# ScalarE loads one table set for Exp and Ln, and other sets at written places, in a two-block transformer kernel

## The reference

```
rms_norm:        x * rsqrt(mean(x*x) + eps) * g           (Sqrt; or Ln, then Exp)
recurrence:      log_f = logaddexp(log_lb, log1p(-lb) + log_sigmoid(fr))
                 k_in  = (1 - lb) * sigmoid(-fr)           (Exp, Ln; Sigmoid)
                 decay = exp(differences of cumsum(log_f))  (Exp)
attention:       softmax                                    (Exp)
stick-breaking:  log_beta = log_sigmoid(z)
                 log_1m   = where(mask, log_sigmoid(-z), 0)
                 after    = cumsum(log_1m, reverse) - log_1m
                 a        = exp(log_beta + after)           (Exp, Ln; Exp)
feed-forward:    (silu(h @ w_gate) * (h @ w_up)) @ w_down   (Silu)
gates:           sigmoid(...)                               (Sigmoid)
rotary tables:   cos, sin                                   (Sin)
```

## Time and profile before

| | before |
|---|---|
| median of 3 runs | 1090.27 us (1089.99 to 1090.49) |
| span of the profiled execution | 1087.6 us |
| TensorE (PE) busy | 1062.6 us, 98% |
| VectorE (DVE) busy | 748.0 us, 69% |
| ScalarE (ACT) busy | 599.6 us, 55% |
| table loads (ACT_TABLE_LOAD) | 36, 46.2 us |

### The profile page before, as it was taken

One profiled execution on the slowest core, in us unless ns is written; L12 is line 12 of the kernel. 1 busy time (PEld: TensorE's weight loads), 2 busy tenths in 40 slices (PEclk: granted clock), 3 DMA queues, 4 the chain that ended last, 5 costly groups with the idle time before them and its releaser, 6 DMA issues.

```text
span 1087.6 us, 22291 instructions
## 1 busy us (share of the span) xinstructions
PE 1062.6 (98%) x8792; PEld 1030.8 (95%) x8792; DVE 748.0 (69%) x1103; ACT 599.6 (55%) x896; POOL 75.0 (7%) x89
## 2 busy tenths in 40 slices
PE   7999999999999999999999999999899999999998
PEld 6899898999999999999999999988898999999998
DVE  6889798647776665567666667657667776666566
ACT  3555755476565554556555445464766565554454
POOL 0001000000320000021000001050000310000010
PEclk8999999999999999999999999999999999999999
DMA  6455434334555554565655456554334455555563
GB/s 211 143 165 174 155 117 136 141 111 166 189 185 203 193 193 157 187 200 192 216 193 193 147 190 220 174 175 160 112 117 154 164 187 198 192 194 176 187 222 117
DMA packets 32300, 187.81 MB, mean 173 GB/s; under 512 B 3816, under 2 KB 7536, under 8 KB 14448
## 3 DMA queue, kind: packets, MB, share of 16 engines
q1 hardware_dynamic: 31328, 185.58, 49.5%
q0 software_dynamic: 416, 1.06, 0.4%
q10 hardware_dynamic: 496, 0.33, 0.2%
HBM read 184.98 MB, written 1.06 MB: 171 GB/s over the span
## 4 chain that ended last, share of the span: by engine, by line
PE 83%; DVE 11%; ACT 3%; issue 1%; DMA 0%; DVEq 0%; ACTq 0%
PE acc L633 78%; DVE wlo L1494 4%; PE area_t L633 3%; PE area_a L633 2%; ACT whi L1124 1%; ACT s_a L1124 1%; DVE s_sum L2050 1%; DMA posi<-in_pos 0%; DVE st L1680 0%; ACT f_p L1124 0%; PE area_t L897 0%; DVE score L1722 0%; DVE f_sc L1942 0%; DVE work L1735 0%; DVE st L1733 0%
## 5 line engine op out<-in xcount | busy, mean ns | idle before, releaser
L633 PE MATMUL acc<-hs,whi 128*128 128x256 f32 x3584 | 624.0, 279 | 7.1 <-DVE wlo L1494 5.9
L633 PEld LDWEIGHTS acc<-hs,whi 128*128 128x128 f32 x3584 | 541.7, 187 | 13.8 <-issue 7.5
L633 PE MATMUL acc<-hs,wlo 128*128 128x256 f32 x1792 | 496.9, 277 | 0.0
L1124 ACT ACTIVATE whi<-raw 128x1024 fp32r<-128x1024 f32 (+3 forms) x379 | 356.6, 977 | 156.9 <-PE acc L633 130.8
L1494 DVE TENSOR_TENSOR wlo<-raw,whi 128x1024 fp32r<-128x1024 f32 (+4 forms) x259 | 272.5, 1094 | 109.1 <-ACT whi L1124 108.2
L633 PEld LDWEIGHTS acc<-hs,wlo 128*128 128x128 f32 x1792 | 336.3, 188 | 0.2
L633 PE MATMUL acc<-hid,whi 128*128 128x256 f32 x1056 | 180.7, 277 | 0.2 <-DVE wlo L1494 0.2
L633 PEld LDWEIGHTS acc<-hid,whi 128*128 128x128 f32 x1056 | 159.3, 188 | 0.4 <-DVE wlo L1494 0.4
L633 PE MATMUL acc<-hid,wlo 128*128 128x256 f32 x528 | 146.0, 277 | 0.0
L1581 DVE TENSOR_TENSOR wlo<-raw,whi 128x1024 fp32r<-128x1024 f32 x120 | 141.2, 1219 | 3.8 <-ACT whi L1124 3.7
L1594 DVE TENSOR_TENSOR hbuf<-acc,sbuf 128x256 f32<-128x256 f32 x66 | 28.0, 425 | 116.5 <-PE acc L633 113.1
(11 more groups left out here) (317 smaller groups left out, 1061.1 us busy)
## 6 DMA issues: line engine op xcount, KB each, us to landing
raw<-in_w_gu SPq DMA_DIRECT2D x66, 1024.0 KB, 4.8
raw<-in_w_dn SPq DMA_DIRECT2D x48, 704.0 KB, 4.0
raw<-in_w_up SPq DMA_DIRECT2D x10, 1024.0 KB, 4.8
raw<-in_w_gates1b SPq DMA_DIRECT2D x8, 1024.0 KB, 4.8
raw<-in_w_out SPq DMA_DIRECT2D x8, 1024.0 KB, 4.8
raw<-in_w_qk SPq DMA_DIRECT2D x8, 1024.0 KB, 4.9
raw<-in_w_gates SPq DMA_DIRECT2D x8, 1024.0 KB, 4.8
raw<-in_w_projT_b SPq DMA_DIRECT2D x7, 1024.0 KB, 4.8
```

Of the source, the lines that this page charges most:

```text
L633: return nc.tensor.matmul(out, w, m, start=start, stop=stop, skip_group_check=True)
L1124: return nc.scalar.activation(out, in_, f, **kw)
```

## The change

The loads stand: before the wait of every `mean_root`, with one for Silu's set right behind the root in the three feed-forwards; around the two Sin; at `bound0`, on both sides of the recurrence's Sigmoid, at `hgrn_n`, `hgrn_gate`, `log_forget`, and before three of the five gate Sigmoids. The rule that puts loads in by itself stays as it was, and puts none where the set loaded last has the function.

```diff
+SIGMOIDS, ROOTS, EXP_AND_LN, SINES, SILUS = 2, 3, 6, 9, 18
...
+            def load_set(functions):
+
+                nc.scalar.add_instruction(mybir.InstLoadActFuncSet(
+                    act_func_set_id=functions, name=nc.get_next_instruction_name(),
+                    engine=mybir.EngineType.Activation))
...
             def mean_root(name):
 
+                load_set(ROOTS)
                 act.wait_ge(S("t_full"), TURN_T[name] + 1)
...
                     fn(xr[:], area_t[:, 0, :], ACT.Sqrt, scale=1.0 / D, bias=epsb[:, 0:1]).then_inc(S("t_freed"), 1)
+                if name in ("norm1", "norm2", "norm5"):
+                    load_set(SILUS)
...
                 elif name == "tables":
+                    load_set(SINES)
                     act.wait_ge(S("angles"), 1)
                     fn(sin[:], rest[:], ACT.Sin).then_inc(S("sines"), 1)
                     fn(cos[:], over[:], ACT.Sin).then_inc(S("sines"), 1)
+                    load_set(EXP_AND_LN)
...
                 elif name == "bound0":
+                    load_set(EXP_AND_LN)
                     act.wait_ge(S("lb_diff"), 1)
...
                 elif name == "decay_xc":
+                    load_set(SIGMOIDS)
                     act.wait_ge(S("decay_sum"), 1)
                     fn(hk[:], flat(bf[:, :, :]), ACT.Sigmoid, scale=-1.0).then_inc(S("key_sig"), 1)
+                    load_set(EXP_AND_LN)
...
                 elif name == "hgrn_n":
+                    load_set(EXP_AND_LN)
                     act.wait_ge(S("t_full"), TURN_T[name] + 1)
...
                 elif name == "hgrn_gate":
+                    load_set(SILUS)
                     act.wait_ge(S("copied"), LEFT_PSUM[BLOCKS["bg"] + 3][1])
...
                 elif name.startswith("gate_sigmoid"):
                     first_block, b = name[12] == "1", int(name[14])
+                    if name in ("gate_sigmoid1_0", "gate_sigmoid1_1", "gate_sigmoid2_0"):
+                        load_set(SIGMOIDS)
...
                 elif name == "log_forget":
+                    load_set(EXP_AND_LN)
                     act.wait_ge(S("forget_in"), 1)
```

## The result

| | before | after |
|---|---|---|
| median of 5 runs | 1090.15 us (1089.32 to 1090.49) | 1084.17 us (1083.24 to 1084.70) |
| ratio, with its 95% interval | | 0.9947 (0.9935 to 0.9959) |
| span of the profiled execution | 1087.6 us | 1082.6 us |
| ScalarE busy | 599.6 us | 580.9 us |
| table loads | 36 | 21 |

The kernel after is 6.0 us faster, some 0.5%. The forecast was 1084.3 us. The two profiled executions are only 5.0 us apart. In every run with both on record the time stands 1.74 to 1.87 us above the span.

The account below looks back on a forecast made before the run. TensorE, busy 98%, was taken to bound the kernel, with ScalarE's table loads costing only where it waits behind them; 0.96 + 5.07 = 6.0 us off 1090.27 gave 1084.3 us, range 1083.2 to 1086.9.

Parts of the forecast that it names:

- Five loads on the chain: Removed loads at 110.8, 727, 748, 767 and 812 us, between Exp and Ln, each worth 1.27 us of the chain.
- eleven beside it: The other eleven of 16 removed loads: worth nothing, as engines behind them wait for TensorE or have queued work.
- First stretch: Recurrence, load at 110.8 us: TensorE gains 0.96 us, its wait for `wlo`, and is then bound by itself.
- Second stretch: Second block's attentions, four loads from 727 to 812 us: TensorE's waits shrink and it ends 5.07 us earlier.
- Loads ahead of the waits: Loads already stood ahead of their activations' waits, so writing them there moves nothing: 0 us.
- What is moved: Three feed-forwards, Silu's load goes ahead of the next `whi`, which comes 1.4 us later but is covered: 0 us.
- repeat the pattern: The other two feed-forwards were taken to be covered like the first, where VectorE slips some 0.15 us: cost 0.
- The load behind the Sigmoid: Recurrence, it delays the `whi` at 132.34 us by 1.4 us, still ahead of VectorE's split at 136.56: 0.
- Set 6: Exp and Ln's common set, never loaded before; taken as no dearer, with 0 to 1.6 us at risk.
- other wait ended last: Rival, chance 0.12: something the chain doesn't show holds TensorE's waits; gain only 3.1 us, about 1087.2 us.
- The written loads were seen: Against a rival, chance 0.04: the placing rule misses written loads, 36 stay and 20 are added, 1092.8 us.
- The drain: Rival, chance 0.03: a removed switch frees more than its load, some 1380 ns of drain; gain 9.0 us, 1081.3.

Follow-up runs that it names:

- e4: Kernel after the change, with Exp and Ln's set loaded again at the five places the prediction put on the chain; 1089.93 us, ratio 1.0004 to the kernel before.
- e6: Kernel after the change, with fifteen more loads, one behind each of 15 weight-tile splits in the first feed-forward; 1083.43 us, ratio 0.9943 to the kernel before.
- e9: Kernel after the change, with the Sigmoid's load moved up behind the recurrence's second Ln; 1082.88 us, 1082.62 us once more, ratio 0.9937 to before both times.
- e2: Kernel after the change, with all written loads taken out but Exp and Ln's set at `log_forget`; 1084.39 us, ratio 0.9951 to the kernel before.
- e3: Kernel after the change, without any written load of Exp and Ln's set, the other sets' loads kept; 1089.55 us, ratio 1.0000 to the kernel before.
- e8: Kernel after the change, with one more load behind the wait in each of the four `sb_x` steps; 1085.46 us, ratio 0.9958 to the kernel before.
- e11: Kernel after the change itself, run once more on one chip with the kernel before; 1083.83 us, ratio 0.9943 to the kernel before.
- e10: As e4, with one more load ahead of Exp in four Exp-then-Ln pairs, nine on the chain; 1095.77 us, ratio 1.0060 to the kernel before.

## Why the prediction was right

- *Five loads on the chain, eleven beside it.* Shown from both sides: e4 has the five and not the eleven, and is as slow as the kernel before; e6 adds fifteen covered ones, at other places than the eleven, and loses nothing that its interval shows.
- *First stretch, 0.96 us.* Segment A says 0.92. The limit was TensorE's wait, not the load's 1.27, as put. Not as put is that TensorE "is then bound by itself": the chain still holds it at 137 us, by 0.51 us of idle time after (0.39 before), and e9 takes that.
- *Second stretch, 5.07 us.* Segment C says 4.99, and e2 has it with one line. The steps within it hold too: after 770 us the sum left 4.16 - 3.81 = 0.35 us of wait, and 0.39 is there; the waits at 781 and 784 were to stay, and did (0.80 and 0.53 us of idle time against 1.00 and 0.53). At 820 the sum left 1.98 - 1.27 = 0.71: 0.58 is there. Only at 733 the sum took all of 1.24 and 0.23 stayed, which the chain made up for at the next waits; and the list of what to look for, "no wait near 768", contradicted the sum, which has one there.
- *Loads ahead of the waits, 0.* e3 shows it to within 1 us, and its segments A and C (187.68 and 234.87) are those of the kernel before. e8 shows what a load held behind its wait would have cost; the earlier trace rows had shown one of the kernel before's that isn't held.
- *What is moved, 0.* Right in the first feed-forward, wrong in the second by 0.25 us. In the first the load now stands ahead of `whi`, where the earlier trace rows had it behind:

```profile
317.50 1.28 ACT L1155 ACT_TABLE_LOAD   x1
318.79 2.01 ACT L1125 ACTIVATE whi<-raw 128x1024 fp32r<-128x1024 f32 x2
```

  and VectorE's split, in its timeline, waits 0.16 us for it, where 0.15 was put against the earlier trace rows:

```profile
319.88 2.36 DVE L1514 TENSOR_TENSOR wlo<-raw,whi 128x1024 fp32r<-128x1024 f32 x2 [0.16 <-ACT whi L1125]
```

  The prediction then said that the others "repeat the pattern". In the second, VectorE also waits 0.16 us (at 502.95), but the kernel before had only some 0.2 us in hand there: the first half of its `wlo` is done at 504.41 (an estimate: the start, 503.26, plus 1.15), and TensorE starts on it at 504.64. TensorE's timeline at this place, before and after:

```profile
504.52 0.28 PE L633 MATMUL acc<-hs,wlo 128*128 128x256 f32 x1
504.64 0.40 PE L633 MATMUL acc<-hs,whi 128*128 128x256 f32 x2
504.87 0.28 PE L633 MATMUL acc<-hs,wlo 128*128 128x256 f32 x1
```

```profile
503.97 0.28 PE L634 MATMUL acc<-hs,wlo 128*128 128x256 f32 x1
504.23 0.51 PE L634 MATMUL acc<-hs,whi 128*128 128x256 f32 x2
504.58 0.28 PE L634 MATMUL acc<-hs,wlo 128*128 128x256 f32 x1
```

  From one `wlo` row to the next it is 0.35 us before and 0.61 after. The profile prints no idle time for it: the two delays, 0.14 us ahead of the `whi` row and 0.11 inside it, are each under the 0.16 us by which a record overlaps the next start. Only the starts show them. The third feed-forward shows no such step: from the wait at 848 us (852.81 before, 847.75 after) to the start of the last matmul it is 231.36 us before and 231.37 after.

- *The load behind the Sigmoid, 0.* Right: in the chain shown with e9, VectorE comes to `wlo` at 135.28 out of its own work, not out of a wait for the `whi` that the load delays. What the prediction didn't price is the load in front of the Sigmoid, a sixth one on the chain, which the change keeps; it left the sum as it was, and e9 takes it.
- *Set 6, as dear as the others.* Its load takes 1.283 us, and its Exp and Ln 0.63.
- *The rivals.* No other wait ended last in the two stretches. The written loads were seen: 21 in the trace (19 of them written, where the rival counted 20). The drain: by the Trainium skill (page "ScalarE: Activation LUTs", section "What ACT_TABLE_LOAD costs") each switch to a different set costs some 1380 ns more than the load. The trace doesn't agree. The four loads on the chain in segment C of the kernel before and of e3 are such switches, and C is 234.90 and 234.87 with them, 229.95 in the mean without: 1.24 each. The four that e4 puts back there are loads of the set that is in already, and cost 235.02 - 229.95 = 5.07 us, 1.27 each. No run here shows the drain.
- *The numbers.* The sum of 6.03 us stands 0.37 above the 5.66 of the segments: 0.25 in the second feed-forward, 0.04 in the first stretch, 0.08 in the second. That the medians differ by just 6.0 us is in part luck, since the interval of the ratio reaches 1.3 us to either side and e11, on one chip with its kernel before, is 5.3 us faster. The 2.7 us that the prediction put between span and median are no fixed distance (it is 1.8 within one run, the rest is scatter), but they drop out of the difference.

## What to carry to other kernels

Price a table load by its place, not by its count: on the chain that TensorE waits behind, as between Exp and Ln, it costs its 1.28 us or as much of them as TensorE waits (0.96 in the first stretch), and nothing where ScalarE would wait anyway. One load of a set that holds both functions, written once ahead of the stretch, is most of the change: e2 has 5 of the 6 us with one line. When a load is written by hand, ask what stands ahead of it in ScalarE's queue, not only which wait it is put before: moving the Sigmoid's load above a copy that waits for TensorE was worth 0.7 us more. And when a load is moved ahead of work that others wait for, check the time in hand at each place where the pattern repeats: what was free in one feed-forward cost 0.25 us in the next, where only 0.2 us were in hand.

## What the runs showed of the hardware

- **Behind three waits of TensorE of over 2 us the granted clock fell.** The waits are of 2.07 us (e8, 777.90) and of 2.08 and 2.17 us (e10, 119.43 and 775.52); the clock fell to 0.5 for 3.4 us each time, beginning 0.3 to 1.1 us after work had begun again. Waits of 1.43 us, which every trace has near 176 us, and of 1.76 and 1.97 us (e10, 756.86 and 824.46) brought no fall. Whether the length of the wait alone decides isn't shown. Half of 3.4 us is lost at most, 1.7 (an estimate). e8's segment C lost 2.2 where 0.6 was expected, though much of the fall lay over the multiplications of ones, whose results nobody reads: they stand in TensorE's queue ahead of the attention's. The first fall of e10 cost 1.5 us, the second nothing that its segment shows.
- **Loading the set that is already loaded** costs the same 1283 ns as a switch (e4).
- **Matmuls run at two spacings at a granted clock of 1.00.** The same tile of 48 matmuls took 5.66 us in the profiled execution before and 5.48 us in the one after, 118 and 114 ns a matmul (the chain of work that ended last, from 718.69 before and 718.84 after). How long either lasts differs from one execution to the next, also of one kernel (B is 329.25 us after and 328.57 in e11, the same kernel), and TensorE has next to no idle time in B that could make the difference. Why it changes was not tried and is open.
